# Attention heads: scores one round ahead, biases added in the window of the exponentials, three score buffers

## The reference

```
scores = einsum(q, k) * 128 ** -0.5
scores = where(valid, scores - slope[g, h] * |distance|, -1e30)
m = max(scores); e = exp(scores - m); den = sum(e)
o = einsum(e, v) / den;  lse = m + log(den)
alpha = softmax(lse over the 3 groups)
merged = sum(alpha * o)
```

## Time and profile before

| what | value |
| --- | --- |
| median of 3 runs | 3436.28 us (3436.12 to 3440.94) |
| the profiled execution's own time | 3443.07 us |
| its span, first to last instruction | 3441.3 us |
| mean granted TensorE clock | 0.947 of full speed |
| PE busy | 3071.6 us (89%) |
| DVE busy | 1414.7 us (41%) |
| ACT busy | 1084.2 us (32%) |
| stretch of the stage's rounds | about 1115 to 1192 us |

### The profile page before, as it was taken

How to read it: one execution, slowest core, us unless ns; L and a number is a source line. 1 busy time by engine, 2 the same in 40 slices (tenths; PEclk the granted TensorE clock), 3 DMA queues, 4 the chain that set the end, 5 groups by cost and what they waited for, 6 DMA issues and landing times. The chain is left out here.

```text
span 3441.3 us, 54813 instructions
## 1 busy us (share of the span) xinstructions
PE 3071.6 (89%) x24140; PEld 2390.4 (69%) x24140; DVE 1414.7 (41%) x2665; ACT 1084.2 (32%) x1737; POOL 318.5 (9%) x464
## 2 busy tenths in 40 slices
PE   6888887888898788879999889999899998898998
PEld 5777676433788643347777667777687876677998
DVE  5455555321444641243333343333433324435554
ACT  4344443211443321132222223222232223234443
POOL 0122221211000011100001010000000000000000
PEclk9889988999999999989999999999999999999999
DMA  6333323799665169944543233443232222203453
GB/s 261 118 112 115 128 106 139 283 411 413 253 221 205 51 233 414 415 185 172 181 154 141 86 110 147 154 170 129 74 110 92 98 80 104 86 25 122 156 182 104
DMA packets 113629, 580.06 MB, mean 169 GB/s; under 512 B 24048, under 2 KB 26608, under 8 KB 60400
## 3 DMA queue, kind: packets, MB, share of 16 engines
q1 hardware_dynamic: 66160, 449.96, 34.6%
q0 software_dynamic: 47232, 126.60, 10.3%
HBM read 669.79 MB, written 1.05 MB: 195 GB/s over the span
## 5 line engine op out<-in xcount | busy, mean ns | idle before, releaser
L352 PE MATMUL ps<-t,t 128*128 128x512 f32 (+1 forms) x3488 | 1221.8, 350 | 114.1 <-DVE t L552 52.9
L353 PE MATMUL ps<-t,t 128*128 128x512 f32 (+1 forms) x3488 | 1210.5, 347 | 0.0
L354 PE MATMUL ps<-t,t 128*128 128x512 f32 (+1 forms) x3488 | 1209.2, 347 | 0.0
L329 DVE TENSOR_TENSOR t<-t,t 128x1024 fp32r<-128x1024 f32 x448 | 550.6, 1233 | 778.3 <-ACT t L310 778.1
L352 PEld LDWEIGHTS ps<-t,t 128*128 128x128 f32 x3488 | 667.3, 191 | 223.1 <-issue 69.7
L354 PEld LDWEIGHTS ps<-t,t 128*128 128x128 f32 x3488 | 667.3, 191 | 85.8
L353 PEld LDWEIGHTS ps<-t,t 128*128 128x128 f32 x3488 | 668.1, 192 | 82.0
L310 ACT ACTIVATE t<-t 128x1024 fp32r<-128x1024 f32 x448 | 470.1, 1055 | 587.7 <-PE ps L354 578.9
L1408 PE MATMUL ps<-t,t 128*32 128x512 f32 x1504 | 224.6, 617 | 40.4 <-DMA t<-in_experts_dram,t 34.2
L692 POOL DMA_DIRECT2D t<-in_wmod_dram x224 | 119.0, 537 | 1212.2 <-PE ps L641 1032.8
L1408 PEld LDWEIGHTS ps<-t,t 128*32 128x32 f32 x1504 | 55.4, 112 | 185.3 <-issue 112.6
(11 more groups left out here) (311 smaller groups left out, 2970.5 us busy)
## 6 DMA issues: line engine op xcount, KB each, us to landing
t<-in_wall_dram SPq DMA_DIRECT2D x221, 1024.0 KB
t<-in_experts_dram SPq DMA_DIRECT2D x192, 1024.0 KB
t<-in_wmod_dram POOLq DMA_DIRECT2D x224, 512.0 KB, 5.8
t<-in_wmod_dram SPq DMA_DIRECT2D x16, 512.0 KB, 12.9
t<-in_wall_dram SPq DMA_DIRECT2D x10, 512.0 KB
t<-in_lora_dram POOLq DMA_DIRECT2D x8, 512.0 KB, 3.9
t<-in_rcst_dram POOLq DMA_DIRECT2D x1, 1536.0 KB, 6.8
t<-in_experts_dram,t POOLq DMA_INDIRECT x90, 11.4
```

The costliest lines, as they stand in the source:

```text
L329: e.tensor_tensor(lo, self.raw(n), hi, ALU.subtract).then_inc(*net.wlo.up((self.name, n)))
L352: e.matmul(out, lh, rh, start=start, stop=False, **kw)
L353: e.matmul(out, lh, rl, start=False, stop=False, **kw)
L354: return e.matmul(out, ll, rh, start=False, stop=stop, **kw)
```

## The change

Three edits in `AttnHeads`, nothing elsewhere. The buffers S are three in place of two, and S[n % 3] replaces S[n % 2] everywhere; biased n then waits for turn n-3 in place of turn n-2. PE computes score 0 ahead of the loop, and score n+1 in round n, where score n stood. DVE adds biased 0 ahead of the loop, and in round n it adds biased n+1 between peak n and the wait for exp n. The banks rotate over all eight during the stage. ACT's list is the same but for the buffers.

```diff
-        self.S = [f(768) for _ in range(2)]
+        self.S = [f(768) for _ in range(3)]
...
+    def pe_score(self, e, w, n):
+        net, h, i = self.net, n // 2, n % 2
+        net.banks.take(w, ("score", n, 0))
+        net.banks.take(w, ("score", n, 1))
+        for g in range(3):
+            m = e.matmul(self.out(n, g), net.q[g][:, h, 128 * i:128 * i + 128], net.kk_[g][:, h, :], start=True, stop=True)
+        m.then_inc(*net.sums.up(("score", n)))
...
     def pe(self, e, w):
         net = self.net
-        net.banks.rot = [2, 3, 4, 5, 6, 7]
+        self.pe_score(e, w, 0)
         for n in range(18):
-            if n < 16:
-                h, i = n // 2, n % 2
-                net.banks.take(w, ("score", n, 0))
-                net.banks.take(w, ("score", n, 1))
-                for g in range(3):
-                    m = e.matmul(self.out(n, g), net.q[g][:, h, 128 * i:128 * i + 128], net.kk_[g][:, h, :], start=True, stop=True)
-                m.then_inc(*net.sums.up(("score", n)))
+            if n < 15:
+                self.pe_score(e, w, n + 1)
             if n > 1:
                 self.pe_values(e, w, n - 2)
             if 0 < n < 17:
                 self.pe_turn(e, w, n - 1)
-        net.banks.rot = list(range(8))
...
     def dve(self, e, w):
         net = self.net
         w.wait_ge(net.s_ac, 16)
+        self.dve_biased(e, w, 0)
         for n in range(18):
             if n < 16:
-                h, i, Sn = n // 2, n % 2, self.S[n % 2]
-                w.wait_ge(*net.sums.of(("score", n)))
-                if n > 1:
-                    w.wait_ge(*net.sums.of(("turn", n - 2)))
-                for g in range(3):
...
+                Sn = self.S[n % 3]
                 w.wait_ge(*net.vecs.of(("biased", n, 2)))
                 e.tensor_reduce(self.nm[:, n:n + 1], Sn, AX.X, ALU.max, negate=True).then_inc(*net.vecs.up(("peak", n)))
+                if n < 15:
+                    self.dve_biased(e, w, n + 1)
                 w.wait_ge(*net.acts.of(("exp", n)))
...
+    def dve_biased(self, e, w, n):
+        net, h, i, Sn = self.net, n // 2, n % 2, self.S[n % 3]
+        w.wait_ge(*net.sums.of(("score", n)))
+        if n > 2:
+            w.wait_ge(*net.sums.of(("turn", n - 3)))
+        for g in range(3):
+            slope = float(2.0 ** (-8.0 * (8 * g + h + 1) / 24))
+            d = self.dist[:, 768 * i + 256 * g:768 * i + 256 * g + 256]
+            e.scalar_tensor_tensor(out=Sn[:, 256 * g:256 * g + 256], in0=d, scalar=-slope, in1=self.out(n, g),
+                                   op0=ALU.mult, op1=ALU.add).then_inc(*net.vecs.up(("biased", n, g)))
```

More of the change, by code:

```diff
@@ L2550, in pe_turn @@
         for y in range(6):
-            m = e.transpose(self.turned(n, y), self.S[n % 2][:, 128 * y:128 * y + 128], net.c("ident"))
+            m = e.transpose(self.turned(n, y), self.S[n % 3][:, 128 * y:128 * y + 128], net.c("ident"))
         m.then_inc(*net.sums.up(("turn", n)))
@@ L2600, in act @@
             if n < 16:
-                Sn = self.S[n % 2]
+                Sn = self.S[n % 3]
                 w.wait_ge(*net.vecs.of(("peak", n)))
@@ L2643, in dve @@
                 net.banks.emptied(("turn", m, 1), net.vecs, ("turned", m))
+    def dve_biased(self, e, w, n):
[8 more added lines that the diff above has]
+                                   op0=ALU.mult, op1=ALU.add).then_inc(*net.vecs.up(("biased", n, g)))
+        net.banks.emptied(("score", n, 0), net.vecs, ("biased", n, 1))
+        net.banks.emptied(("score", n, 1), net.vecs, ("biased", n, 2))
 class AttnOut(Stage):
```

## The result

The changed kernel takes 3414.94 us in the median (3408.06 to 3417.16, 6 runs), the kernel before 3436.2 us beside it (3434.23 to 3443.7). The ratio is 0.9932, with a 95% interval of 0.9918 to 0.9946. It is faster, by 21.3 us; 16.1 were forecast, and 3414.94 lies 2.1 us under the lower end of the stated range.

The account below looks back on a forecast made before the run. The prediction took the attention-head stage to be bound by DVE's chain through ACT's exponential, with no engine full. It summed 16.65 - 0.3 - 0.25 = 16.1 us less, 3436.28 to 3420.2 us, range 3417.0 to 3426.0.

Parts of the forecast that it names:

- The chain and its hole: Attention-head rounds: DVE's own work sets the 4.42 us round, but for 1.09 us in which DVE waits for ACT's exponential.
- 15 x 1.11 = 16.65 us: Between the 16 maxima: additions move into the hole, each of 15 intervals falls from 4.42 to 3.31 us, saving 16.65 us.
- The tight fit, 0.3 us: DVE's additions end just 0.03 us before the reciprocal could start; a late start costs 0.3 us over 15 rounds.
- the cover: Additions beside the exponential: hidden without slowing, since copies of DVE and ACT and the scaling already run side by side unstretched.
- The first rounds: Start of the stage: round 2's additions wait once for scores computed at the lower clock, a loss of 0.25 us.
- PE has 0.07 us to spare: PE in the changed round: its work takes 3.24 us from starts against 3.31, leaving 0.07 us before the next values.
- T: Start of DVE's maximum in a round, from which the forecast counts offsets; the next maximum was put at T + 3.31.
- the first rival: Rounds: PE becomes the bound at 3.53 us at most, gain 13.35 us, time 3422.9 us; chance 0.11.
- What follows moves as a whole: Behind the stage: expert weights are issued right after its last instruction, so later transfers start earlier by the same amount.
- The tail behind the last maximum keeps its order: End of the stage, behind the last maximum: its order stays as it was, with no gain or loss set down.
- the scatter: Scatter of whole-kernel runs, which spread over 4.8 us: some 2.6 us taken off for the range's lower end.
- The value of 0.2%: Whole kernel: 0.2% (6.9 us) is about what a measurement can tell from no change; chance of a larger gain 0.93.

Follow-up runs that it names:

- two buffers: The changed kernel with two score buffers in place of three: 3437.11 us in the median (10 runs), ratio 1.001 to the kernel before.
- scores not ahead: The changed kernel, but PE computes score n in round n as before: 3467.31 us in the median (4 runs), ratio 1.0098 to the kernel before.
- PE's part alone: The kernel before with scores one round ahead and eight banks, DVE's order and two buffers unchanged: 3435.24 us (10 runs), ratio 1.0.

## Why the prediction was wrong in its range and right in its mechanism

- **The chain and its hole** were read rightly. The kernel with two buffers and the one with scores not ahead came out with the round lengths that the same offsets gave (4.83 us, and 6.06 in the rounds at the upper clock), and the kernel with PE's part alone showed that the scores were never late before.
- **15 x 1.11 = 16.65 us** was the likely sum of the rounds: the maxima span 50.8 us in place of 67.0 (16.2). In four profiles of the changed kernel they span 50.2 to 51.2.
- **The tight fit, 0.3 us**, was not paid. The additions start 0.86 us behind the maximum's start, not 0.95, as rows of DVE overlap by that much; they end 0.1 us before the reciprocal starts. What was said for the cover beforehand was read too widely: in the earlier trace rows only the scaling runs beside ACT's copy, and DVE's own copy starts at 1137.53, after that one has ended at 1137.22.
- **The first rounds** cost more than was said: the additions of round 3 wait 0.23 us for scores, as forecast, but the values behind them run partly at the lower clock (2.00 us in place of 1.50), and the round takes 3.96 us, 0.66 over a steady one where 0.25 were set down.
- **PE has 0.07 us to spare** was too much. Its round is 3.29 us, not 3.24. The first rounds leave it late, its values start 0.65 us behind T and not 0.23, and it makes up about 0.01 us per round. It came out harmless by luck of 0.01 us: the first rival was as good as true in its mechanism, at 3.29 us in place of 3.53. The Trainium skill, Perfetto Trace Analysis, section "Identifying the Most-Contended Engine", calls the busy time of matmuls no good measure of how close PE is to its limit and takes that of LDWEIGHTS as one of two in its place. In the round of the earlier trace rows neither gives the 3.29 us: weight loads stand at 3.05, which is 0.24 short, and matmul records at 3.53, 0.24 over.
- **What follows moves as a whole** was right in its order: the first expert weights are issued at 1167.55, right behind the stage's last instruction at 1167.13. (They were expected near 1176; the stretch ahead of the stage was 7.2 us shorter in that profile.)
- **The step that failed** is the one from the sum to the range. It put everything outside the rounds at nothing ("The tail behind the last maximum keeps its order", "What follows moves as a whole"), and it put the scatter at 2.6 us. The rounds, the only part that was priced, gave 16.3 us where 16.1 were forecast. The stage as a whole gave 17.7 us by the mean of the profiles: 0.3 more before its first maximum and 1.1 in its tail. The tail is 14.5 us in both kernels where the clock stays up, but 16.0 in the mean of three profiles of the kernel before (14.5, 17.7, 15.7) and 14.9 in the changed kernel's four (14.5, 16.0, 14.5, 14.5), because in some executions the clock falls there, in the changed kernel's one case only at the start of the projection. PE pauses for 2.19 us in the old tail, and the values behind this pause ran below the upper clock in two profiles of three; in the changed kernel the same pause is 1.07 us. What lies outside the stage gave another 2.8 to 4.2 us over all comparisons, and 6.2 in the first, where the means are 23.9 us apart. How much of this is scatter and how much the kernel's own stays open.
- **The scatter** was judged from three runs that spread over 4.8 us. Over all comparisons the runs of the kernel before spread from 3421.7 to 3448.7, with a standard deviation of 5.3 us, of which 2.3 are left once the mean clock is taken out by the fit. In the profiles most of it lies in the stretch ahead of the stage (1092.0 to 1111.1 us in the seven profiles of these two kernels) and little behind it (2240.0 to 2243.9). From that deviation, as an estimate, a mean of three runs is uncertain by 3.1 us and one of six by 2.2, so 2.6 us was too little for a difference of the two.

The value of 0.2% that was given as what a measurement can tell apart was fair for single comparisons of some ten runs: their intervals reach 0.12 to 0.15% to each side.

## What to carry to other kernels

When an engine waits for another inside a round, look for work of the next round that only lacks a buffer, and price the move with offsets from one start in the trace; such offsets held here to a few hundredths of a microsecond, in three different orders, wherever the clock stayed at its upper level. Then add up the other engines' rounds from starts: the gain ends where the next of them is full, and here that was at once. Before giving a range, take the scatter from more than three runs, and ask whether a difference lies in the stretch that was changed: the stretch ahead of the stage, which nobody touched, differs by 16 us between three profiles of one kernel (1095.4 to 1111.1).

## What the runs showed of the hardware

The second profile of the kernel before (first score at 1111.1) shows the clock falling where the first did not. In the busy time by stretch, its stretch from 1184 to 1192 stands at 0.79, in the rounds' tail, where the first profile stands at 1.00.

```profile
1184.00:1192.00 8.00, 5.57 (x34) 5.11 (x32) 3.07 (x8) 2.16 (x6) 0.00 (x0) 0.79 0.00 0
```

The values behind PE's pause there, in the first profile and in the second:

```profile
1186.74 1.58 PE L2560 MATMUL ps<-t,t 128*128 128x128 f32 x12 [2.19 <-DVE t L2642]
```

```profile
1187.89 2.76 PE L2560 MATMUL ps<-t,t 128*128 128x128 f32 x12 [2.19 <-DVE t L2642]
```

The same instructions behind the same pause of 2.19 us ran at the upper level in one execution and at the lower one in the other. So the length of one pause does not decide it alone.

Pauses of 0.89 us in each round of 4.42 us (the kernel before) and of 1.30 us in each round of 4.83 us (two buffers) left the clock at its upper level in the steady rounds. Pauses of 2.53 us in rounds of 6.06 us (scores not ahead) did so in every second round only. The Trainium skill, TensorE: Matmul & The Clock Gate, section "A second HAM failure mode: psum-queue depth-cycling", tells of such swings in a kernel that cycles through PSUM banks with short pauses between groups. Here the cycling alone did not bring them: the changed kernel, two buffers and scores not ahead all rotate over eight banks, and only the last, with the longest pauses, swung in its rounds.

An exponential on ACT and additions on DVE that read PSUM and SBUF ran side by side with the durations they have alone, within 0.01 us.
